# Splitting the first expert matrix on GpSimd, and routing the last token tile from rows that are not normed yet

## What is computed

```python
hx = _rmsnorm(x, norm2[l]) * (1.0 + cx2) + sx2
s = jax.nn.sigmoid((xf @ w_router).astype(jnp.float32))
sb = (s + router_bias).reshape(T, N_GROUPS, EXPERTS_PER_GROUP)
group_score = lax.top_k(sb, 2)[0].sum(-1)
gsel = jnp.argmax(group_score, axis=-1)
...
_, loc = lax.top_k(in_group, TOP_K)
wts = wts / jnp.sum(wts, axis=-1, keepdims=True)
...
return (jax.nn.silu(xblk @ w1[e]) * (xblk @ w3[e])) @ w2[e]
```

## Time and profile before

| | |
|---|---|
| median of 3 runs | 911.49 us |
| the profiled execution, its own time | 911.87 us |
| its span in the profile | 910.1 us |
| PE busy | 873.1 us, 96% of the span |
| DVE busy | 631.4 us, 69% |
| ACT busy | 408.1 us, 45% |
| POOL busy | 186.3 us, 20% |
| DMA | 195.86 MB, mean 215 GB/s |

### The profile page before, as it was taken

The page is one execution under the profiler, slowest core; times in us unless marked ns, Lnnn a source line. Parts: engine busy times, 40 slices in busy tenths (PEclk is TensorE's granted clock), DMA queues, the critical chain, the costliest instruction groups (busy, mean ns, idle before and its releaser), DMA issues.

```text
span 910.1 us, 15878 instructions
## 1 busy us (share of the span) xinstructions
PE 873.1 (96%) x5819; PEld 746.4 (82%) x5820; DVE 631.4 (69%) x875; ACT 408.1 (45%) x571; POOL 186.3 (20%) x224
## 2 busy tenths in 40 slices
PE   8999999999999999999899999999999999999982
PEld 6799878888997667887788888888888898888871
DVE  1578745699767657566785577599755736699884
ACT  3584456111225422222524265477542634577761
POOL 4052001100000010110012232234222313142352
PEclk9999999999999999999779999999999999999996
DMA  9956456511035123223966969799979668699994
GB/s 343 338 171 188 130 154 203 154 47 47 1 140 186 51 90 115 74 102 137 362 237 187 313 194 353 224 337 377 370 247 318 198 194 292 182 348 369 367 324 146
DMA packets 81958, 195.86 MB, mean 215 GB/s; under 512 B 4398, under 2 KB 12787, under 8 KB 81914
## 3 DMA queue, kind: packets, MB, share of 16 engines
q1 hardware_dynamic: 70656, 158.87, 49.2%
q0 software_dynamic: 8384, 26.39, 11.9%
q10 hardware_dynamic: 2874, 10.01, 2.8%
HBM read 169.56 MB, written 26.23 MB: 215 GB/s over the span
## 4 chain that ended last, share of the span: by engine, by line
PE 78%; DVE 11%; DMA 4%; issue 3%; POOL 2%; ACT 1%; SPq 0%; ACTq 0%; POOLq 0%; DVEq 0%
PE ps L2266 26%; PE ps L2277 8%; PE ps L1940 8%; PE ps L1943 7%; PE ps L2282 4%; PE ps L2140 2%; PE ps L2260 2%; PE ps L2131 1%; PE ps L2133 1%; PE ps L2132 1%; DMA arena<-x_rows 1%; DVE arena L1320 1%; PE ps L1913 1%; DMA x_rows<-arena,block_dst 1%; PE ps L1996 1%
## 5 line engine op out<-in xcount | busy, mean ns | idle before, releaser
L2266 PE MATMUL ps<-w3h,xTh 128*128 128x256 f32 x368 | 106.0, 288 | 0.0
L2266 PE MATMUL ps<-w3h,xTl 128*128 128x256 f32 x368 | 104.3, 283 | 0.0
L2266 PE MATMUL ps<-w3l,xTh 128*128 128x256 f32 x368 | 104.2, 283 | 0.0
L1712 DVE TENSOR_TENSOR w1l<-raw,w1h 128x2048 fp32r<-128x2048 f32 x30 | 68.6, 2286 | 27.7 <-ACT w1h L1077 27.7
L1077 ACT ACTIVATE w1h<-raw 128x2048 fp32r (+1 forms) x32 | 61.1, 1912 | 56.7 <-PE ps L2282 47.1
L2266 PE MATMUL ps<-w2h,hTh 128*128 128x512 f32 x184 | 77.9, 423 | 3.5 <-DVE hTl L1725 3.1
L1077 ACT ACTIVATE w2h<-raw 128x2048 fp32r (+1 forms) x32 | 61.3, 1920 | 30.9 <-PE ps L2266 24.4
L2277 PE MATMUL ps<-w1h,xTh 128*128 128x512 f32 x184 | 72.4, 393 | 1.1 <-issue 1.1
L2266 PE MATMUL ps<-w2h,hTl 128*128 128x512 f32 x184 | 72.8, 395 | 0.0
L718 POOL DMA_INDIRECT x_rows<-arena,block_dst x21 | 50.5, 2403 | 108.2 <-DVE arena L1730 108.2
L2266 PE MATMUL ps<-w2l,hTh 128*128 128x512 f32 x184 | 72.6, 395 | 0.0
(11 more groups left out here) (376 smaller groups left out, 2158.8 us busy)
## 6 DMA issues: line engine op xcount, KB each, us to landing
...
```

Of the source, the lines that this page charges most:

```text
L1712: dve.tensor_tensor(half_of(j, w_lo[j][:, :], k), half_of(j, raw[:, bass.ds(base, UNIT)], k), half_of(j, w_hi[j][:, :], k).bitcast(F32), A ...
L2266: ins = pe.matmul(out_ap, parts[l][:, lhs], w_parts[w][:, cols], start=start and n == 0, stop=stop and n == 2)
```

## The change

Four things are changed together.

1. The low part of the first expert's w1 is made by POOL (two subtractions of 128x2048 after `table_ready`) and no longer by DVE. DVE's two subtractions for w3 of the first expert stand behind the low part of the first block's rows (`turn_out(0)`), where one stood ahead of it.
2. The logits of the last tile come from its rows before the norm: PE turns x2 itself, the router's weights are multiplied with the scale (`w_late`), and DVE multiplies the product with the row's root and adds a shift, the product of the shift with the router's weights (`logit_shift`). ACT squares the last tile in halves. The normed row is made behind that for the store alone: its product with a2b, then `last_normed(0)` and, behind the choice, `last_normed(1)`. The dummy run `keep_busy(14)` on PE goes.
3. `late_columns` makes `w_late` and the sum for the shift in step t = 1, from a small load and a transposition in step t = 0.
4. The choice is made in three pieces: tiles 0 to 3 in step t = 7 ahead of the normed row of tile 6, tiles 4 and 5 in step t = 8, tiles 6 and 7 at the end. The weights of tiles 4 to 7 and their half of the table of weights are made between `block_tok` and `tables()`.

The diff, cut to its core (unchanged lines are mostly left out, and the sums of semaphore counts that only follow from the added square):

```diff
@@ -565,11 +573,14 @@
             elif first and n == 2:
+                sp.wait_ge(S["hx2_ready"], NX)
+            elif first and n == 3:
                     sp.wait_ge(x2_stored[par], 16 * NX // 2)
-                sp.wait_ge(S["hx2_ready"], NX + 1)
-            elif not (first and n == 3):
+                sp.wait_ge(S["hx2_turned"], 2 * NX)
+                sp.wait_ge(S["ss_ready"], SQ)
+            else:
...
@@ -690,7 +703,13 @@
             pool.wait_ge(S["ss_ready"], NT + u + 1)
-            link(pool, bc, pool.tensor_scalar(stat[:, NT + u:NT + u + 1], stat[:, u:u + 1], 1.0 / D, EPS, ALU.mult, ALU.add))
+            if u < NX - 1:
+                link(pool, bc, pool.tensor_scalar(stat[:, NT + u:NT + u + 1], stat[:, u:u + 1], 1.0 / D, EPS, ALU.mult, ALU.add))
+            else:
+                link(pool, bc, pool.tensor_scalar(stat[:, X0 + 1:X0 + 2], stat[:, X0:X0 + 1], 1.0 / D, EPS, ALU.mult, ALU.add))
+                pool.wait_ge(S["ss_ready"], SQ)
+                link(pool, bc, pool.tensor_scalar(stat[:, NT + u:NT + u + 1], stat[:, u:u + 1], 1.0 / D, stat[:, X0 + 1:X0 + 2],
+                                                  ALU.mult, ALU.add))
...
@@ -735,13 +754,17 @@
-        pool.wait_ge(S["ss_ready"], NT + NX + FIN_ORDER.index(t) + n)
+        pool.wait_ge(S["ss_ready"], SQ + FIN_ORDER.index(t) + n)
     pool.wait_ge(S["table_ready"], 1)
+    for k in range(2):
+        pool.wait_ge(w_high[0], k + 1)
+        pool.tensor_tensor(half_of(0, w1l[:, :], k), half_of(0, raw[:, 0:UNIT], k), half_of(0, w1h[:, :], k).bitcast(F32), ALU.subtract)\
+            .then_inc(w_split[0], 1)
...
@@ -1008,6 +1031,14 @@
+    def row_square(t, h):
+        act.wait_ge(S["x2_ready"], 2 * t + h + 1)
+        act.wait_ge(S["oss_ready"], NX)
+        if h:
+            act.wait_ge(S["ss_ready"], NT + NX)
+        act.activation(square_out, x2_of[t][:, h * HALF:(h + 1) * HALF], ACT.Square,
+                       accum_out=stat[:, t:t + 1] if h else stat[:, X0:X0 + 1]).then_inc(S["ss_ready"], 1)
...
@@ -1034,7 +1064,14 @@
             turned_out(u, 1)
+        if t == NX:
+            row_square(NX - 1, 0)
+        if t == NX + 1:
+            act.dma_start(x_dram[u * P:(u + 1) * P, :], x2_of[u]).then_inc(x2_stored[u % 2], 16)
+        if t >= 2:
             logit_rows(u)
+        if t == NX:
+            scores_out(u)
...
@@ -1049,7 +1086,10 @@
                     wo_row_high(t - 1, k)
-        if 1 <= t <= NX:
+        if t == NX:
+            turned_out(NX - 1, 0)
+            row_square(NX - 1, 1)
+        elif t >= 1 and t < NX:
...
@@ -1061,15 +1101,13 @@
             act.dma_start(x_dram[w * P:(w + 1) * P, :], x2_of[w]).then_inc(x2_stored[w % 2], 16)
-        if u == NX - 1:
-            act.wait_ge(S["hx2_ready"], NX + 1)
-            act.dma_start(hx_dram[u * P:(u + 1) * P, :], hx2[:, u % 2, :]).then_inc(hx2_stored[u % 2], 16)
-        if t >= 2:
+        if 2 <= t < NX:
             scores_out(u)
+    act.wait_ge(S["late_logits"], 1)
+    act.activation(score[:, NX - 1, :], score[:, NX - 1, :], ACT.Sigmoid).then_inc(S["rl_out"], 1)
+    act.wait_ge(S["hx2_ready"], NX + 2)
+    act.dma_start(hx_dram[(NX - 1) * P:NX * P, :], hx2[:, (NX - 1) % 2, :]).then_inc(hx2_stored[(NX - 1) % 2], 16)
     act.wait_ge(S["rl_out"], NX)
-    for par in range(2):
-        act.wait_ge(x2_stored[par], 16 * NX // 2)
-    act.wait_ge(S["hx2_ready"], NX + 1)
...
@@ -1463,7 +1501,17 @@
-    EARLY = NX - 2
+    EARLY, FIRST = NX - 2, NX - 4
+    def late_columns():
+        dve.wait_ge(S["small_turned"], 2)
+        cols = ps[:, 7, 0:16]
+        dve.tensor_tensor(shift_terms.rearrange("p (k e) -> p k e", k=KC), w_rt[:, :, 0:NE],
+                          cols[:, 0:KC].unsqueeze(2).broadcast_to([P, KC, NE]), ALU.mult)
+        v(dve.scalar_tensor_tensor(out=gain_columns, in0=cols[:, KC:], scalar=1.0, in1=small[:, 24:32], op0=ALU.add, op1=ALU.mult))
+        dve.tensor_tensor(w_late, w_rt[:, :, :], gain_columns.unsqueeze(2).broadcast_to([P, KC, RANK2]), ALU.mult)
+        dve.tensor_reduce(shift_sum, shift_terms.rearrange("p (k e) -> p e k", k=KC), AX.X, ALU.add).then_inc(S["small_ready"], 1)
...
@@ -1549,10 +1598,11 @@
                 wo_row_low(1, k)
+        if t == 1:
+            late_columns()
         if t == NX:
-            clear_counts()
-            early = choose(0, EARLY)
-            for _ in early:
+            weights(0, FIRST)
+            for _ in choose(FIRST, EARLY):
...
@@ -1585,27 +1635,47 @@
             residual(u, 1)
-            if u == NX - 1:
-                weights(0, EARLY)
             gated_low(t)
-        if t >= 1:
+        if t == NX - 1:
+            clear_counts()
+            for _ in choose(0, FIRST):
+                pass
+        if 0 <= u < NX - 1:
             dve.wait_ge(S["pow_ready"], NT + u + 1)
-            for cols in [slice(0, D)] if u < NX - 1 else [slice(0, HALF), slice(HALF, D)]:
-                link(dve, sc, dve.scalar_tensor_tensor(out=hx2[:, u % 2, cols], in0=x2_of[u][:, cols],
-                                                       scalar=stat[:, 2 * NT + u:2 * NT + u + 1],
-                                                       in1=a2b[:, cols], op0=ALU.mult, op1=ALU.mult))
-                dve.tensor_tensor(hx2[:, u % 2, cols], hx2[:, u % 2, cols], s2b[:, cols], ALU.add).then_inc(S["hx2_ready"], 1)
+            link(dve, sc, dve.scalar_tensor_tensor(out=hx2[:, u % 2, :], in0=x2_of[u], scalar=stat[:, 2 * NT + u:2 * NT + u + 1],
+                                                   in1=a2b, op0=ALU.mult, op1=ALU.mult))
+            dve.tensor_tensor(hx2[:, u % 2, :], hx2[:, u % 2, :], s2b, ALU.add).then_inc(S["hx2_ready"], 1)
+    end = NX - 1
+    root = stat[:, 2 * NT + end:2 * NT + end + 1]
+    def last_normed(h):
+        cols = slice(h * HALF, (h + 1) * HALF)
+        dve.scalar_tensor_tensor(out=hx2[:, end % 2, cols], in0=hx2[:, end % 2, cols], scalar=root, in1=s2b[:, cols],
+                                 op0=ALU.mult, op1=ALU.add).then_inc(S["hx2_ready"], 1)
+    dve.wait_ge(S["x2_ready"], 2 * NX)
+    dve.tensor_tensor(hx2[:, end % 2, :], x2_of[end], a2b, ALU.mult).then_inc(S["hx2_ready"], 1)
+    dve.wait_ge(S["small_turned"], 3)
+    dve.tensor_copy(logit_shift, ps[:, 4, 0:NE]).then_inc(S["small_ready"], 1)
+    dve.wait_ge(S["hx2_ready"], NX)
+    dve.wait_ge(S["pow_ready"], NT + NX)
+    last_normed(0)
+    dve.wait_ge(S["small_ready"], 3)
+    dve.wait_ge(S["logit_done"], NX)
+    dve.scalar_tensor_tensor(out=score[:, end, :], in0=ps[:, 7, P:P + NE], scalar=root, in1=logit_shift, op0=ALU.mult, op1=ALU.add)\
+        .then_inc(S["late_logits"], 1)
         pass
-    weights(EARLY, NX)
+    last_normed(1)
...
@@ -1673,31 +1743,27 @@
             .then_inc(S["slots_done"], 1)
-    for k in range(2):
-        is_blk = slotw[:, k * NX:(k + 1) * NX, :]
-        v(dve.tensor_tensor(is_blk, is_blk, R["wk"][:, k, :].unsqueeze(2).broadcast_to([P, NX, NB]), ALU.mult))
-    dve.sem_inc(S["slots_done"], 1)
+    def weigh_slots(first_tile, end):
+        for k in range(2):
+            is_blk = slotw[:, k * NX + first_tile:k * NX + end, :]
+            v(dve.tensor_tensor(is_blk, is_blk, R["wk"][:, k, first_tile:end].unsqueeze(2).broadcast_to([P, end - first_tile, NB]), ALU.mult))
+        dve.sem_inc(S["slots_done"], 1)
+    dve.wait_ge(S["slots_done"], 2)
+    weigh_slots(0, FIRST)
                              op0=ALU.add, op1=ALU.add).then_inc(S["tok_ready"], 1)
+    weights(FIRST, NX)
+    weigh_slots(FIRST, NX)
     dve.sem_inc(S["table_ready"], 1)
-    for k in range(2):
-        dve.wait_ge(w_high[0], k + 1)
-        dve.tensor_tensor(half_of(0, w1l[:, :], k), half_of(0, raw[:, 0:UNIT], k), half_of(0, w1h[:, :], k).bitcast(F32), ALU.subtract)\
-            .then_inc(w_split[0], 1)
+    last = dve.value_load(tabs[0:1, T_LAST:T_LAST + 1], min_val=NE - 1, max_val=MAXB - 1)
         dve.wait_ge(hx2_stored[par], 16 * NX // 2)
-    dve.wait_ge(w_high[1], 1)
-    dve.tensor_tensor(half_of(1, w3l[:, :], 0), half_of(1, raw[:, UNIT:2 * UNIT], 0), half_of(1, w3h[:, :], 0).bitcast(F32), ALU.subtract)\
-        .then_inc(w_split[1], 1)
-    dve.wait_ge(S["rank_done"], 3)
-    v(dve.tensor_copy(slot_w[:, :], ps[:, 5, 0:NB]))
-    last = dve.value_load(tabs[0:1, T_LAST:T_LAST + 1], min_val=NE - 1, max_val=MAXB - 1)
...
@@ -1737,7 +1803,10 @@
     turn_out(0)
+    low(1, UNIT, 0, 0)
     low(1, UNIT, 0, 1)
+    dve.wait_ge(S["rank_done"], 3)
+    dve.tensor_copy(slot_w[:, :], ps[:, 5, 0:NB])
...
@@ -2153,16 +2222,19 @@
         bank = h if u == NX - 1 else 7
+        rows_ = x2_of[u] if u == NX - 1 else hx2[:, u % 2, :]
         if u == NX - 1:
-            pe.wait_ge(S["hx2_ready"], u + h + 1)
+            pe.wait_ge(S["x2_ready"], 2 * u + h + 1)
                 pe.wait_ge(S["rl_out"], u)
+            else:
+                pe.wait_ge(S["small_ready"], 2)
         for k in range(4):
```

(22 more changed lines are left out.)

41 lines of the change are left out of this document (26 added, 15 removed).

## The result

The changed kernel takes 916.93 us in the median of 10 runs (914.90 to 917.59); the kernel before, run beside it, 911.78 (911.05 to 915.05). The ratio is 1.0039 with a 95% interval of 1.0027 to 1.0052: slower by some 3.6 us, about twice what such a measurement can tell from no change. The two medians lie further apart, by 5.2 us, because seven of the ten runs of before took 911.05 to 912.77 and three 914.5 to 915.1; the means of the runs give 1.0042. I had forecast 912.9, between 909.6 and 915.8. The ratio puts the kernel at 915.3, inside the range and near its end; the median of its own runs lies 1.1 us beyond the end. The profiled execution took 917.04 us (span 915.2), 5.2 more than that of before.

A forecast was written before the change was run, and what follows sets the result against it. PE, busy 96% of the span, was taken to bound the kernel, so shifts ahead of the experts move the end. 911.87 + 1.25 (hidden half) + 0.15 (small transposition) = 913.3, or 912.9 for the median; range 909.6 to 915.8.

The forecast's parts named there:

- The last tile: Last tile's logits: residual ends 2.5 us later, shorter chain behind it, so the last choice begins 2.2 us earlier, at 440.1.
- GpSimd's speed: First expert's w1 split on POOL: two subtractions of 4.6 us each from 459.8, the middle of 2.29 and 6.9.
- The two rivals with another speed: POOL's w1 halves at 6.9 us each: 917 (0.14 together with being overtaken); or at 2.3 to 2.8: 909.4 (0.15).
- Who holds whom: POOL's w1 split holds DVE: the first w3 half, ready to start at 464.9, waits until 469.05.
- the rival without it (911.7): GpSimd doesn't hold DVE: w3 and w2 early, second gather late, 0.6 gained to 0.9 lost, about 911.7; chance 0.13.
- The hidden half: First expert's hidden half reaches PE's transposition at 478.55, 1.25 us later than before, behind DVE's held w3 and w2.
- The step that failed: the second gather: Second gather, behind POOL's split: issued about 472.1, landing 7.9 us later at worst, 480.0, before PE's want at 480.2.
- The rival that came true on top: the clock: A 2.4 us stall of PE at 476 lowers its clock, adding 1.7 us: 914.6; chance 0.20.
- the likeliest case: POOL's halves take 4.6 us and hold DVE, clock stays up: 912.9 median, own range 911.9 to 913.9; chance 0.38.
- its own sign: The prediction counts as wrong if, among other signs, PE's clock falls once more behind 475 us.
- The rival in which DVE gets in ahead of POOL's second half: DVE does one w3 half before POOL's second w1 half: 2.3 us more, about 915; 0.14 together with slow GpSimd.
- The parts that I listed: Chances: forecast 0.38, a third above 913.3; clock 0.20; slow or overtaken GpSimd 0.14; no hold 0.13; fast GpSimd 0.15.

The follow-up runs named there:

- dve_split: The changed kernel with both low halves of the first w1 made by DVE behind the tables, none by GpSimd; 910.15 us, ratio 0.9976.
- gather_between: The changed kernel with the second gather issued on GpSimd between the two halves of the w1 split, not behind both; 916.35 us, ratio 1.0039.
- order_alone: The kernel before with only DVE's order at the start of the first expert as in the changed kernel; 912.75 us, ratio 1.0000.
- pool_split_alone: The kernel before with only the first w1's split moved to POOL and DVE's order behind it as in the changed kernel; 916.75 us, ratio 1.0044.
- fillers: The changed kernel with dummy products of PE ahead of the hidden transposition and the turned block, in block 0 alone; 916.05 us, ratio 1.0037.
- two_pieces_pool: The changed kernel, w1's split still on POOL, with the choice in two pieces (tiles 0 to 5, then 6 and 7); 915.47 us, ratio 1.0026.

## Why the prediction was nearly right

**The last tile.** Forecast: residual at 436.5, last choice at 440.1. Measured 436.51 and 439.85. I gave this part 2.2 us by itself, and dve_split gains 2.2. That the figures agree so well is luck: in its trace the gather comes 3.3 us earlier, not 2.2 (2.3 to 3.4 in the six kernels with this routing and three pieces), and the interval of its ratio reaches from 0.7 to 3.7 us.

**GpSimd's speed.** Forecast 4.6 a half from 459.8. Measured 4.5 (9.04 for two) from 459.22. The middle of two bounds held, but I had no mechanism for it, so that is luck. The Trainium skill, GPSIMD Engine Reference, section 3.1, gives 4497 ns for an addition of this size; the trace agrees for the subtraction (9.04 us for two). The two rivals with another speed are out.

**Who holds whom.** Forecast: DVE's w3 is held until POOL's second half ends. Shown: 8.22 us against 4.48 in dve_split, and 8.68 for w2 in gather_between, where w3 isn't held; in both DVE is through 4.35 us behind POOL's end. The rule of the Trainium skill, SBUF — State Buffer, section "Who interferes with whom", is confirmed for the direction that no row of before showed; the rival without it (911.7) is out.

**The hidden half.** Forecast 1.25 us late at its transposition; it was 0.20. The tables were 0.6 us earlier than I had them and POOL's end came at 468.27, not at 469.0, so that DVE's two w3 halves ended at 472.62, 0.9 earlier than the 473.5 that I had. An error of 1.05 us, on the cheap side.

**The step that failed: the second gather.** Forecast: it "is issued at about 472.1 and lands 7.9 us later at worst, at 480.0, where PE wants it at 480.2". Shown: it was issued at 471.27, landed 9.89 us later, at 481.16, and at the full clock PE would have wanted it at 479.16. The 7.9 was the longest of the gathers in the earlier trace rows, and I used it as an upper bound. It is none: the same gather took 8.4 us in order_alone and 8.7 in dve_split with nothing held. Here its issue took 2.21 us beside DVE's subtractions, not 0.98. The others that came behind POOL's whole split landed after 10.16 (pool_split_alone), 9.71 (fillers) and 9.77 us (two_pieces_pool). And the want at 480.2 rested on the hidden half's 1.25 us, of which only 0.20 came true. The step was sized at nothing and is worth 2.0 us: 2.04 in the account above, 1.85 in fillers.

**The rival that came true on top: the clock.** I gave 0.20 to a clock that falls once behind 475 us, and 1.7 us as its price. It fell, and with that the likeliest case failed by its own sign ("wrong [...] if PE's clock falls once more behind 475"). The price is 2.0 us behind the gather's landing, from the account and from fillers. I had named 914.6 for this case; the ratio puts the kernel at 915.3. (The rival in which DVE gets in ahead of POOL's second half, about 915, is as near by its number, but its mechanism didn't occur.) 911.87 + 0.20 + 2.04 + 2.03 + 0.8 for the end makes 916.9, the 917.04 of the profiled execution. The forecast for it was 913.3.

**The chances.** The parts that I listed make slower than 913.3 more likely than I wrote: a third of 0.38, 0.20 and 0.14 are 0.47, not 0.40, which leaves 0.35 within 0.2%, not 0.42. By my own parts slower was the likeliest outcome, and it is what came.

So the shorter way through the last tile, the order of POOL and DVE and the holding of DVE were right, and the time fell into the range by the ratio. The middle was 2.4 us low by the ratio and some 4 by the medians. What it lacked is the gather, taken as just in time, and the clock, taken as unlikely; what made up for part of it is the hidden half, 1.05 us too dear.
